# First block's attention: one ring of three PSUM banks for pieces and turned blocks

## The reference, cut to what matters

```python
q = rotate(q) * (A_QK_DIM ** -0.5)          # two maps of 64 columns per head
k = rotate(k)
sc = einsum('bhcqd,bhckd->bhcqk', q, k)
p = softmax(where(mask, sc, NEG_INF))
w = p[:, :, 0] - lam * p[:, :, 1]
out = einsum('bhqk,bhkv->bhqv', w, vh)
out = rms_norm(out, subln_g) * (1.0 - lam_init)   # then times silu(az)
```

## Time and profile before

| | |
|---|---|
| median of 3 runs | 4174.61 us (4174.05 to 4181.87) |
| the profiled execution | 4179.9 us |
| its span | 4178.1 us |
| TensorE matmuls, busy | 3812.7 us, 91% of the span |
| VectorE, ScalarE, GpSimd, busy | 1788.7, 1090.4 and 1300.0 us |
| granted TensorE clock, mean | 0.954 of full speed |
| attention of the first block | 49 to 443 us and 1313 to 1710 us of the span |

### The profile page before, as it was taken

How to read it: one execution, slowest core, us unless ns; L and a number is a source line. 1 busy time by engine, 2 the same in 40 slices (tenths; PEclk the granted TensorE clock), 3 DMA queues, 4 the chain that set the end, 5 groups by cost and what they waited for, 6 DMA issues and landing times. The chain is left out here.

```text
span 4178.1 us, 45391 instructions
## 1 busy us (share of the span) xinstructions
PE 3812.7 (91%) x16604; PEld 2878.6 (69%) x16604; DVE 1788.7 (43%) x1994; ACT 1090.4 (26%) x1608; POOL 1300.0 (31%) x672
## 2 busy tenths in 40 slices
PE   5888999999997888899999995999799879989988
PEld 3655788887885655688887884777565668766657
DVE  5455112223154545113223145862455459344654
ACT  2334100112211333201102212133355211434551
POOL 1211244442342221244442342443222235232212
PEclk9999999999998999999999997999799889988999
DMA  3000111111122000111111123111101121110102
GB/s 127 27 25 18 43 51 51 45 46 36 36 76 96 26 26 13 40 53 51 45 50 32 38 63 109 46 39 33 29 27 36 51 98 50 33 32 27 31 21 105
DMA packets 63197, 196.40 MB, mean 47 GB/s; under 512 B 7344, under 2 KB 12720, under 8 KB 62512
## 3 DMA queue, kind: packets, MB, share of 16 engines
q1 hardware_dynamic: 51088, 149.74, 12.3%
q10 hardware_dynamic: 11936, 44.31, 2.9%
HBM read 173.05 MB, written 20.97 MB: 46 GB/s over the span
## 5 line engine op out<-in xcount | busy, mean ns | idle before, releaser
L447 POOL TENSOR_TENSOR Whi<-stage,b_credit 128x1024 fp32r<-128x1024 f32 (+2 forms) x332 | 552.0, 1663 | 2781.4 <-PE psA L404 1670.7
L404 PE MATMUL psA<-Hhi,Whi 128*128 128x512 f32 x2944 | 928.9, 397 | 41.0 <-DVE Hlo L1899 40.3
L404 PE MATMUL psA<-Hlo,Whi 128*128 128x512 f32 x2944 | 912.9, 391 | 0.0
L404 PE MATMUL psA<-Hhi,Wlo 128*128 128x512 f32 x2944 | 911.7, 391 | 0.0
L450 POOL TENSOR_TENSOR Wlo<-stage,Whi 128x1024 fp32r<-128x1024 f32 (+2 forms) x332 | 747.5, 2252 | 26.0
L404 PEld LDWEIGHTS psA<-Hhi,Whi 128*128 128x128 f32 x2944 | 554.4, 189 | 179.8 <-ACT Hhi L1797 35.9
L404 PEld LDWEIGHTS psA<-Hlo,Whi 128*128 128x128 f32 x2944 | 556.6, 189 | 117.4
L404 PEld LDWEIGHTS psA<-Hhi,Wlo 128*128 128x128 f32 x2944 | 556.4, 189 | 116.8
L385 PE MATMUL psT<-Hhi,Whi 128*128 128x512 f32 x768 | 342.1, 445 | 118.8 <-DVE Hlo L1240 41.1
L385 PE MATMUL psT<-Hlo,Whi 128*128 128x512 f32 x768 | 324.7, 423 | 0.0
L385 PE MATMUL psT<-Hhi,Wlo 128*128 128x512 f32 x768 | 323.0, 421 | 0.0
(11 more groups left out here) (270 smaller groups left out, 4412.9 us busy)
## 6 DMA issues: line engine op xcount, KB each, us to landing
stage<-in_w SPq DMA_DIRECT2D x216, 512.0 KB, 3.5
xs<-X ACTq DMA_DIRECT2D x4, 4096.0 KB, 13.5
b_wk<-xs ACTq DMA_DIRECT2D x32, 512.0 KB, 3.3
stage<-in_w SPq DMA_DIRECT2D x52, 256.0 KB, 2.6
stage<-in_w SPq DMA_DIRECT2D x32, 384.0 KB, 3.1
b_wk<-in_x SPq DMA_DIRECT2D x8, 512.0 KB, 3.6
rope<-in_ropes ACTq DMA_DIRECT2D x4, 1024.0 KB, 9.9
stage<-in_w SPq DMA_DIRECT2D x32, 128.0 KB, 2.1
```

Of the source, the lines that this page charges most:

```text
L404: mm = pe.matmul(dst[h], w[:, cols], r[k][:, h * HALF:(h + 1) * HALF], start=first and k == order[0] and r is rhi and w is whi, stop=last ...
L447: pool.tensor_tensor(Whi[:, b, 0:n], stage[:, b, 0:n], s.credit[:, 0:1].broadcast_to([P, n]), ALU.add).then_inc(s.w_hi, 1)
```

## The change

Turned blocks and pieces share one ring F of three banks of psT; values have the fourth. A turn of up to four blocks is one use. From q = 4 on a turn is two uses: four blocks, then the rest. Each is filled, waited for and copied by itself. The ring's list of uses is the order of TensorE's program. Since the number of uses need not be a multiple of three, the ring counts the uses of each buffer by itself. A piece that reads what another piece left (sq, sk and vt read RAW, which ScalarE copies from q, k and v) waited for it through the bank before; where the two now lie in different banks it waits for that copy by name. `values` waits for the last use in each bank of those that it needs.

```diff
+def turns(*step):
+    return [("t", *step, part) for part in range(step[-1] // 4 + 1)]
+
 def uses_of_attention(prelude, slots, heads):
-    tp = [(h, q) for h in range(heads) for q in range(NT)]
     av = [(h, g) for h in range(heads) for g in (0, 1)]
-    f = all_pieces(prelude, slots, heads)
-    if ("ss", heads - 2, 1) in f:
-        f.append(("ss", heads - 1, 1))
-    return tp, av, f
+    f = list(prelude)
+    for h in range(heads):
+        for q in range(NT):
+            f += pieces(slots, heads, h, q, 0) + turns(h, q) + pieces(slots, heads, h, q, 1)
+    f.append(("ss", heads - 1, 1))
+    return av, f
...
 class Ring:
-        assert len(uses) % buffers == 0, (name, len(uses))
         self.n, self.buffers = len(uses), buffers
+        self.per = [len(uses[b::buffers]) for b in range(buffers)]
...
+    def last_of(self, *uses):
+        return [max((u for u in uses if self.buf(u) == b), key=self.at.get)
+                for b in sorted({self.buf(u) for u in uses})]
...
-        tp, av, f = uses_of_attention(B1_PRELUDE, B1_SLOTS, HEADS)
-        TP = Ring("b1TP", tp, lambda n: ctx.enter_context(nc.semaphore(n)), 1)
+        av, f = uses_of_attention(B1_PRELUDE, B1_SLOTS, HEADS)
         AV = Ring("b1AV", av, lambda n: ctx.enter_context(nc.semaphore(n)), 1)
-        F = Ring("b1F", f, lambda n: ctx.enter_context(nc.semaphore(n)), 1)
-        psTP, psAV, psF = psT[:, 0], psT[:, 1, 0:HALF], psT[:, 1, HALF:]
+        F = Ring("b1F", f, lambda n: ctx.enter_context(nc.semaphore(n)), 3)
+        psAV = psT[:, 1, HALF:]
+        def bank(use):
+            b = F.buf(use)
+            return psT[:, b // 2, b % 2 * HALF:(b % 2 + 1) * HALF]
...
             def piece(L, use):
...
+                if kind in ("sq", "sk", "vt"):
+                    source = ({"sq": "q", "sk": "k", "vt": "v"}[kind], h, half)
+                    if F.buf(source) != F.buf(use):
+                        pe.wait_ge(*F.drained(L, source))
                 if F.before(use):
                     pe.wait_ge(*F.room(L, use))
...
-                pe.wait_ge(*TP.drained(L, (h, 4 * g + 3)))
-                pe.wait_ge(*F.drained(L, ("vt", h, 1)))
+                for use in F.last_of(("t", h, 4 * g + 3, g), ("vt", h, 1)):
+                    pe.wait_ge(*F.drained(L, use))
...
-                        if TP.before((h, q)):
-                            pe.wait_ge(*TP.room(L, (h, q)))
                         pe.wait_ge(*mixed.upto(L, h * NT + q + 1))
-                        turn(psTP, PR[q % 2][0], q + 1).then_inc(TP.filled_sem, 1)
+                        for use in turns(h, q):
+                            k0 = 4 * use[-1]
+                            pe.wait_ge(*F.room(L, use))
+                            turn(bank(use), PR[q % 2][0][:, k0 * P:], min(4, q + 1 - k0)).then_inc(F.filled_sem, 1)
...
-                        act.wait_ge(*TP.filled(L, (h, q)))
-                        act.activation(WT[:, 0:q + 1, (q % 4) * P:(q % 4 + 1) * P],
-                                       psTP[:, 0:(q + 1) * P].rearrange("p (k c) -> p k c", c=P),
-                                       ACT.Copy).then_inc(TP.freed((h, q)), 1)
+                        for use in turns(h, q):
+                            k0, k1 = 4 * use[-1], min(q + 1, 4 * use[-1] + 4)
+                            act.wait_ge(*F.filled(L, use))
+                            act.activation(WT[:, k0:k1, (q % 4) * P:(q % 4 + 1) * P],
+                                           bank(use)[:, 0:(k1 - k0) * P].rearrange("p (k c) -> p k c", c=P),
+                                           ACT.Copy).then_inc(F.freed(use), 1)
```

More of the change, by code:

```diff
@@ L244, in drained @@
         u = self.at[use]
-        return self.drained_sem[u % self.buffers], L * (self.n // self.buffers) + u // self.buffers + 1 + j
+        return self.drained_sem[u % self.buffers], L * self.per[u % self.buffers] + u // self.buffers + 1 + j
     def before(self, use):
@@ L253, in room @@
         u = self.at[use]
-        return self.drained_sem[u % self.buffers], L * (self.n // self.buffers) + u // self.buffers + j
+        return self.drained_sem[u % self.buffers], L * self.per[u % self.buffers] + u // self.buffers + j
     def freed(self, use):
         return self.drained_sem[self.at[use] % self.buffers]
+    def last_of(self, *uses):
+        return [max((u for u in uses if self.buf(u) == b), key=self.at.get)
+                for b in sorted({self.buf(u) for u in uses})]
 class Tally:
@@ L644, in piece @@
                 kind, h, half = use
-                c = slice(half * HALF, (half + 1) * HALF)
+                c, psF = slice(half * HALF, (half + 1) * HALF), bank(use)
                 if kind in ("q", "k", "v", "z"):
```

## The result

The changed kernel takes **4105.1 us** (median of 4 runs, 4101.6 to 4108.4). The kernel before, run beside it, took 4178.2 (4174.1 to 4184.7). The ratio is 0.982, with an interval of 0.9805 to 0.9842: 73 us faster. In three later comparisons the kernel before had medians of 4174.8, 4170.4 and 4174.1 us; against about 4174 the gain is 69 us, still more than was forecast. The two profiled executions are 4102.4 us (span 4100.5) and 4179.9 us (span 4178.1).

A forecast was written before the change was run, and what follows sets the result against it. TensorE, working in program order, was held by waits for the one bank psF. Waits removed 49 us, idle-column tail +4, new waits -2, prelude clock -1: together 50 us, so 4125 us, range 4112 to 4146.

The forecast's parts named there:

- The waits that go and stay: Both attention stages: waits for the bank vanish except three per kind in heads 0 to 2; 24.5 us per layer, 49 in two.
- the inherited hole: Step q = 3, heads 1 and 2: k(h+1,1) inherits the swap's wait for the Ln of ss, some 2.9 us.
- 0 as my value: k piece behind the 2.9 us hole, heads 1 and 2: clock falls there again, so no gain or loss from it.
- The bound was 9 us, for the pair alone, and a rival: Swap and k piece at q = 3, heads 1, 2: clock stays up, 9 us more, 4116 us; chance 0.10.
- The small term of -1: Both preludes: q1 starts while the clock is low, so its 0.8 us are worth half; -1 us.
- that rule: Skill's rule that short idles while going round PSUM banks swing the clock; read as predicting a time slower than before.
- I take 0.1: Nineteen waits per layer: each gives 0.0 to 0.2 us beyond the idle column, taken as 0.1; 4 us.
- The new waits, -2: TensorE's queue: about 40 added waits per layer, 4 us if none hides, 0 if all do; 2 taken.
- The slack of 0.98 us: Head 0 of layer 1, turn at q = 3: mix(3) ended 0.98 us before it; no new wait taken.
- I am wrong if L609 waits for L1066 in heads 0 to 2: Sign against the forecast: turns in heads 0 to 2 wait for the mix.
- a mean clock well off 0.94: Sign against the forecast: layer 0's mean granted clock differs clearly from the 0.94 of the profile before.
- The other rivals: Gain partly taken back by mix (0.15, 4145 us); all back (0.03, 4175); clock falls in staying holes, slower (0.04, 4185).

## Why the prediction was wrong

The waits that go were right. The sum was too small by its terms for the clock, for the tail of the idle column and for the new waits.

**The waits that go and stay.** Right, in number and in place: five lines gone, 3, 5 and 3 waits left in the others, the inherited hole 2.98 us long. Restoring the waits restored the stages' time. The prelude gave 11 us a layer instead of some 8, heads 1 and 2 gave 8.1 and 7.6 in layer 0 and 9.3 and 9.9 in layer 1 instead of 5 to 7.

**The clock, "0 as my value".** This is the first step that failed, and the largest. "The clock should fall there again" came true only in layer 0, and for a third of the old time at head 1. Counted from the starts of the projections' matmuls, which follow each other by 0.23 us at full clock and by 0.43 at half: the extra spacing in the two stages was 18.5 + 18.9 us before and is 13.1 + 10.6 after. **14 us** of the gain are the clock's: some 6 in the four steps q = 3, some 4 in the preludes, where it recovers sooner, some 2 at head 0's start, where it stays low for 3.4 us instead of 6.8, and the rest in a step 7 of each layer. With all old waits back the extra spacing is 34.5 us again. The bound was 9 us, for the pair alone, and a rival; it was not thought of that shorter holes shorten the low stretches elsewhere. The small term of -1 had even the wrong sign: it took the low stretch at the start of the preludes as given and counted q1's hole there at half its worth. Without that hole the clock came back some 3 to 5 us sooner.

The preludes show it: with a hole of about 1 us before the pieces the clock stayed low for 24.8 to 27.2 us from the stage's start in five of six (before, and the two runs with these waits back; the sixth is 20.9), and for 20.8 and 21.5 in the changed kernel (20.7 to 23.9 in the other experiments whose traces record it). The Trainium skill (TensorE: Matmul & The Clock Gate, section on psum-queue depth-cycling) ties such swings to going round the banks and to TensorE's short idles between groups of matmuls. Here it is one bank that brought the short idles, and going round three that took them away. As the prediction read that rule, the changed kernel would have lost. The runs disagree with it as a rule on rotating; they agree that short idles cost clock.

**The tail of the idle column, "I take 0.1".** The second step that failed. A wait that the column gives as 1.43 us (the q piece at step 1) saved 1.67 to 1.75. With 0.25 us in place of 0.1 the 38 waits give 9.5 us instead of 4. In the preludes, once their clock is taken off, it is 0.2. The bound taken was 0.2.

**The new waits, -2.** Nothing measurable, by the run that issues them five times.

With these the stages come out: 49 + 9.5 + 0 + 14 = 72.5, against 69.6 measured; the 3 that are too much were not traced further, but step 4 of head 3 is longer by 0.8 us in layer 0, and in head 0 the turn of step 3 waits for the mix, below.

**Outside the stages** 7 us went that no step of the prediction speaks of. In the ten experiments' profiles that part took 2457.5 to 2465.0 us, 2464.5 with all waits restored, against 2467.9 in the one profile of before. It is TensorE's pace in code that is the same in all of them, with the clock at half for 215 to 240 us in the experiments. The profiled execution of before was 5 us above that kernel's usual median of some 4174 us, and the one after 2.7 below its own, so a good part of the 7 us is the choice of these two. But with all waits back the median stayed 6 us below the kernel before. Whether the rest depends on the stages ahead stays open.

**The mix.** The slack of 0.98 us at the turn of step 3 was said to hold since the split moves with the piece. TensorE in head 0 of layer 1, after:

```profile
1360.28 0.65 PE L624 MATMUL psT<-ident,X 128*128 128x128 f32 x4 [0.45 <-DVE X L1088]
```

and VectorE just before it, beside GpSimd's split from 1353.18 to 1357.87:

```profile
1353.84 1.78 DVE L1098 TENSOR_TENSOR b_wk<-b_wk,rope 128x512 f32<-128x512 f32 x1
...
1355.74 2.68 DVE L1100 TENSOR_TENSOR b_wk<-b_wk,b_upad 128x512 f32<-128x512 f32 x1
```

The split now slows the two rope operations ahead of the mix (they take 0.68 and 0.69 us alone) instead of the mix itself, and the turn waits 0.45 us. "I am wrong if L609 waits for L1066 in heads 0 to 2" is thus met, by 0.6 us more of such waits in layer 0 than before (1.1 in four, 0.5 in three). As a sign it was misread from the start, since three such waits stood in the kernel before. It is not the cause of the miss. The other sign, a mean clock well off 0.94, could not be read, since that 0.94 leaves out the low stretch of layer 0's prelude. **The other rivals** did not come: at steps 5 and 6 the holes that stay cost no clock (10.8 and 10.9 us in every head), and not a tenth of the gain came back.

## What to carry to other kernels

Where one bank serves a chain of small pieces, count the uses between a piece and the one whose bank it takes: the waits that go can be listed from that beforehand, and each is worth its idle column plus about a quarter of a microsecond, and more where holes hold TensorE's clock down. Sharing a ring with other users adds their uses to the count: with one bank less the same change lost 27 us. A wait that is inherited rather than removed points at the work that comes late; doing that work at once was worth 23 us more in the stages (30 by the medians), while moving a piece behind others without asking what is queued behind its consumer lost 28 in the stages.

## What the runs showed of the hardware

The granted clock behind the same hole of 2.98 us fell in layer 0 and not in layer 1, in another run the other way round, and in a third in both: 1.6 us for each fall. No run shows what decides it.

VectorE's operations on SBUF took 2.6 to 3.9 times their length beside GpSimd's split: 2.35 and 3.17 us instead of 0.75 and 1.15, and 1.78 and 2.68 instead of 0.68 and 0.69. The first two ended 0.5 and 0.95 us behind GpSimd's two operations. The Trainium skill (SBUF — State Buffer, section "SBUF: two separate sides") has the two engines share a pair of ports, if VectorE's operation reads two inputs from SBUF or runs in a mode that uses both ports; one of them holds the pair for a whole instruction while the other is blocked. These rows agree with it for the operations with two inputs. The first of the mix (0.75 us alone) reads one, and no run shows in which mode.
